# Two of sixteen row gathers per step split in two by the expert's number

## The reference

```python
q = (x @ w_query).reshape(B, T, H, 2, 128)                 # H = 8 heads
s1 = einsum('bthd,nd->bthn', q[..., 0, :], sub_keys_1)     # 128 keys each
s2 = einsum('bthd,nd->bthn', q[..., 1, :], sub_keys_2)
v1, i1 = top_k(s1, 16); v2, i2 = top_k(s2, 16)
cand_s = v1[..., :, None] + v2[..., None, :]
cand_e = i1[..., :, None] * 128 + i2[..., None, :]
top_s, top_pos = top_k(cand_s, 16)
experts = take_along_axis(cand_e, top_pos)                 # 16 of 16384
g = softmax(top_s)
u = expert_down[e]
hdn = gelu(einsum('chkd,cd->chk', u, x))
y = einsum('chk,chkd->cd', g * hdn, expert_up[e])
```

## Time and profile before

| | |
|---|---|
| Median of 3 runs | 864.57 us (864.12 to 865.37) |
| Span of the profiled execution, the time that the sums are made against | 862.9 us |
| PE busy | 755.6 us (88%) |
| DVE busy | 564.1 us (65%) |
| ACT busy | 180.2 us (21%) |
| POOL busy | 575.1 us (67%) |
| Moved by DMA | 308.39 MB, of it 268.47 MB by GpSimd's gathers |

### The profile page before, as it was taken

One profiled execution on the slowest core, in us unless ns is written; L12 is line 12 of the kernel. 1 busy time (PEld: TensorE's weight loads), 2 busy tenths in 40 slices (PEclk: granted clock), 3 DMA queues, 4 the chain that ended last, 5 costly groups with the idle time before them and its releaser, 6 DMA issues.

```text
span 862.9 us, 9305 instructions
## 1 busy us (share of the span) xinstructions
PE 755.6 (88%) x2473; PEld 390.9 (45%) x2473; DVE 564.1 (65%) x1503; ACT 180.2 (21%) x563; POOL 575.1 (67%) x716
## 2 busy tenths in 40 slices
PE   9999999999999879788888888888879797777786
PEld 6988668556554424244333434343434242222232
DVE  3565686239999667676767676666676666765445
ACT  2134455211212021122202030202020202112021
POOL 6886451017767777777777777777777777777770
PEclk9999999999999999999999999999999999999999
DMA  8948450659999999999999999999999999999997
GB/s 304 232 133 243 156 236 5 242 243 363 409 380 410 409 409 409 410 409 410 409 409 410 410 410 409 410 409 409 410 410 410 409 410 409 410 410 410 409 409 292
DMA packets 99487, 308.39 MB, mean 357 GB/s; under 512 B 18504, under 2 KB 23424, under 8 KB 99456
## 3 DMA queue, kind: packets, MB, share of 16 engines
q0 software_dynamic: 73728, 268.47, 78.3%
q1 hardware_dynamic: 24656, 39.39, 13.8%
q10 hardware_dynamic: 1072, 0.16, 0.1%
HBM read 306.41 MB, written 1.05 MB: 356 GB/s over the span
## 4 chain that ended last, share of the span: by engine, by line
PE 27%; DMA 27%; POOL 24%; issue 12%; DVE 8%; ACT 1%; DVEq 0%; ACTq 0%
PE bank L1530 24%; POOL region_w L647 18%; DMA region_w<-in_expert_up,chosen 14%; DMA region_w<-in_expert_down,chosen 11%; POOL gates L647 3%; DMA pool_bd<-in_expert_down,chosen 2%; PE xn_ps L1530 2%; PE bank L1533 2%; DVE region_w L1392 1%; POOL dn_spare L647 1%; POOL pool_bd L647 1%; DMA dn_spare<-in_expert_down,chosen 1%; DVE gates L1392 1%; DVE pool_bd L1392 1%; DVE region_q L1166 0%
## 5 line engine op out<-in xcount | busy, mean ns | idle before, releaser
L1530 PE MATMUL bank<-region_w,pool_bd 128*128 128x512 f32 (+2 forms) x1006 | 473.1, 598 | 96.6 <-DMA region_w<-in_expert_up,chosen 89.2
L1530 PEld LDWEIGHTS bank<-region_w,pool_bd 128*128 128x128 f32 x1006 | 174.4, 189 | 366.4 <-issue 294.5
L647 POOL DMA_INDIRECT region_w<-in_expert_up,chosen x250 | 234.8, 939 | 82.7 <-issue 61.4
L1392 DVE CUSTOM_DVE_ANT_0 region_w<-xn_ps,region_w 128x1024 f32<-128x1024 f32 x128 | 156.6, 1224 | 101.4 <-DMA region_w<-in_expert_down,chosen 101.0
L647 POOL DMA_INDIRECT region_w<-in_expert_down,chosen x128 | 120.6, 943 | 40.8 <-issue 32.9
L1392 DVE CUSTOM_DVE_ANT_0 gates<-xn_ps,gates 128x1024 f32<-128x1024 f32 x64 | 78.1, 1223 | 36.7 <-DMA gates<-in_expert_down,chosen 33.1
L908 ACT ACTIVATE pool_bd<-ident,pool_bd 128x128 f32<-128x128 f32 x251 | 78.4, 389 | 77.2 <-PE bank L1530 53.8
L647 POOL DMA_INDIRECT gates<-in_expert_down,chosen x64 | 60.4, 943 | 23.4 <-issue 16.5
L711 ACT ACTIVATE pool_bd<-bank 128x256 f32<-128x256 f32 (+3 forms) x49 | 19.0, 389 | 265.5 <-PE bank L1530 241.3
L1530 PE MATMUL bank<-region_q,oT 128*128 (+1 forms) x240 | 54.3, 379 | 0.0
L1392 DVE CUSTOM_DVE_ANT_0 dn_spare<-xn_ps,dn_spare 128x1024 f32<-128x1024 f32 x32 | 39.2, 1224 | 18.8 <-DMA dn_spare<-in_expert_down,chosen 18.6
(11 more groups left out here) (289 smaller groups left out, 786.8 us busy)
## 6 DMA issues: line engine op xcount, KB each, us to landing
region_q<-in_w_in SPq DMA_DIRECT2D x4, 2048.0 KB, 8.4
region_q<-in_w_query SPq DMA_DIRECT2D x1, 6144.0 KB, 23.9
region_w<-in_expert_up,chosen POOLq DMA_INDIRECT x250, 13.9
region_w<-in_w_out SPq DMA_DIRECT2D x1, 3072.0 KB, 20.9
x_sb<-in_x SPq DMA_DIRECT2D x4, 512.0 KB, 4.0
region_q<-in_w_in SPq DMA_DIRECT2D x2, 1024.0 KB, 11.4
region_q<-in_w_in SPq DMA_DIRECT2D x16, 128.0 KB, 3.0
region_w<-in_wb_nsa SPq DMA_DIRECT2D x2, 1024.0 KB, 16.6
```

The lines of the kernel that those rows point to most:

```text
L647: pool.indirect_dma_start(out=row, out_offset=None, in_=table, in_offset=bass.IndirectOffsetOnAxis(ap=of_slot(chosen, s, k), axis=0)).then ...
L1392: dve.tensor_tensor_reduce(out=row, in0=xn_ps[:, :], in1=row, scale=1.0, scalar=0.0, op0=ALU.mult, op1=ALU.add, accum_out=hdn[:, k:k + 1]) ...
L1530: return pe.matmul(out_, lhsT, rhs, start=start, stop=stop)
```

## The change

The down rows of ranks 7 and 15 (the last place of the ring, `APART`) are fetched in steps 0 to 14 by two gathers instead of one. Both go to the same buffer and count on the same semaphore. The first uses the old list of numbers with the bound 12287: rows of experts up to there are fetched, the others are left out. The second uses a list of its own, `chosen_high`, in which each number under 12288 has 65536 added, and the bound 16383: it fetches just the rows that the first left out. It is issued six downs later (`BEHIND`), after GpSimd has waited for the first one's landing. The dot waits for both. VectorE makes the second list by three small operations for each of the two ranks. In step 15 (`LAST`) all gathers are single as before. The semaphore counts of that place are changed to fit.

```diff
+APART = RING - 1
+BEHIND = 6
+LOW_KEYS = 96
+LOW_ROWS = LOW_KEYS * NK
+BEYOND = 65536.0
...
+        chosen_high = sb("chosen_high", STEPS * 2, U32)
+        high_f = sb("high_f", 4)
...
+        def high_of(s, k):
+
+            return chosen_high[:, bass.ds(s * 2 + k // RING, 1)]
...
-            return (dn_in if low else up_in)[slot], 16 * count
+            return (dn_in if low else up_in)[slot], 16 * (count + (2 * LAST if low and slot == APART else 0))
...
+            def part(index, bound):
+                pool.indirect_dma_start(
+                    out=ring_dn[APART], out_offset=None, in_=a["expert_down"],
+                    in_offset=bass.IndirectOffsetOnAxis(ap=index, axis=0),
+                    bounds_check=bound, oob_is_err=False).then_inc(dn_in[APART], 16)
...
                 if n >= RING:
                     pool.wait_ge(dn_used, n - RING + 1)
-                gather(ring_dn[k % RING], dn_in[k % RING], a["expert_down"], k, s)
+                if k % RING != APART or s == LAST:
+                    gather(ring_dn[k % RING], dn_in[k % RING], a["expert_down"], k, s)
+                else:
+                    part(of_slot(chosen, s, k), LOW_ROWS - 1)
+                first = n - BEHIND
+                if 0 <= first < LAST * SLOTS and first % RING == APART:
+                    pool.wait_ge(dn_in[APART], 32 * (first // RING) + 16)
+                    part(high_of(first // SLOTS, first % SLOTS), NK * NK - 1)
...
+            def high(p, k):
+
+                own.mark(dve.tensor_scalar(out=high_f[:, 0:1], in0=r12[:, 0, k:k + 1], scalar1=float(LOW_KEYS), scalar2=BEYOND,
+                                           op0=ALU.is_lt, op1=ALU.mult))
+                own.mark(dve.scalar_tensor_tensor(out=high_f[:, 1:2], in0=r12[:, 0, k:k + 1], scalar=float(NK), in1=r12[:, 1, k:k + 1],
+                                                  op0=ALU.mult, op1=ALU.add))
+                own.wait()
+                link(dve.tensor_tensor(out=high_of(p, k), in0=high_f[:, 0:1], in1=high_f[:, 1:2], op=ALU.add))
...
                 own.wait()
+                high(p, ranks.stop - 1)
...
+                for k in (RING - 1, SLOTS - 1):
+                    high(p, k)
                 dve.scalar_tensor_tensor(out=of_step(chosen, p), in0=r12[:, 0, :], scalar=float(NK), in1=r12[:, 1, :],
                                          op0=ALU.mult, op1=ALU.add).then_inc(chosen_ready, 1)
...
-            OWN_TURN = 27
+            OWN_TURN = 33
...
-                dve.wait_ge(dn_in[k % RING], (2 * s + k // RING + 1) * 16)
+                turn_ = 2 * s + k // RING + 1
+                if k % RING == APART:
+                    turn_ = turn_ + 2 * LAST if s is LAST else turn_ * 2
+                dve.wait_ge(dn_in[k % RING], turn_ * 16)
```

## The result

The changed kernel takes 994.44 us, median of three runs (993.35 to 994.61), where the kernel before takes 864.57: a ratio of 1.1495 [1.1475, 1.1516], slower by 130 us. The direction was as predicted and the mechanism too, but the size was not: 919 us were predicted and 948 was the upper end. The profiled execution has a span of 992.6 us.

The account below looks back on a forecast made before the run. Before, turns were DMA-bound at 410 GB/s; now the chain binds. d39 at 285.3 + 26 x 22.04 = 858.3, plus 46.9 to the last issue; end 54.4 later, span 917.3, so 919 us; range 886 to 948.

Parts of the forecast that it names:

- The chain: Across GpSimd, DMA and VectorE: first part, 12 gathers, second part, its landing, dot, next first part, with no slack.
- The first turns: Before the steady turns: late dots bring d39 (down gather 39, counted from d0) to about 285 us, where it was 268.35.
- The turn: One round of eight gather pairs: 16.16 + 4.1 + 1.34 + 0.44 = 22.04 us, where it was 20.5.
- L: Second part's time from issue to landing: 4.4 less 0.5 plus 0.2, 4.1 us; bounds 3.1 and 5.6.
- gathers ahead of it still being served, plus 0.2: In the second part's landing time: earlier gathers still on the DMA engines add 0.2 us.
- About 0.1 to start it and let GpSimd go.: Around the late row's dot on VectorE: starting it and releasing GpSimd adds about 0.1 us to its 1.23.
- 13 x 1.243: GpSimd's issues from first to second part: 13 gathers at 1.243 us each, 16.16 us a turn.
- the 0.87 behind slot 15: After a step's last dot, VectorE's other work makes GpSimd lose 0.87 us every second turn, 0.44 on average.
- The DMA engines carry the same bytes.: For the 30 extra gathers: splitting a gather in two adds no bytes for the DMA engines.
- dearer parts: Rival, chance 0.14: skipped rows cost about like real ones, each part 0.3 to 0.6 us dearer; 937 to 955 us.
- is not held: The up gather needing the slot TensorE frees late comes 13.7 us behind the next first part; no wait, costed at nothing.
- The backlog: DMA queue behind GpSimd's issues: it can't build now; last landing lag 5.6 us instead of 16.3, paying back 10.7.

Follow-up runs that it names:

- 7, 6 and 5 pairs: The changed kernel with the second part issued 7, 6 (no edit) or 5 pairs of gathers behind the first: 1068.76, 991.52 and 917.91 us.
- 3 pairs: The changed kernel with the second part issued 3 pairs of gathers behind the first instead of 6: 895.89 us, 1.036 of the kernel before.

## Why the prediction was wrong

The prediction's span was 917.3 us and the trace has 992.6, 75.3 more. By its own steps:

- **The chain.** Right, and shown by the slope with 7, 6 and 5 pairs and by the waits that move with it.
- **The first turns.** d39 was predicted at 285.3. GpSimd's timeline has the first parts of d7, d15, d39 and d239 at

```profile
200.89 1.00 POOL L663 DMA_INDIRECT region_w<-in_expert_down,chosen  x1 [0.30 <-issue]
...
219.76 1.00 POOL L663 DMA_INDIRECT region_w<-in_expert_down,chosen  x1 [3.60 <-DVE pool_bd L1431]
...
291.13 1.00 POOL L663 DMA_INDIRECT region_w<-in_expert_down,chosen  x1 [2.63 <-DVE pool_bd L1431]
...
907.97 1.00 POOL L663 DMA_INDIRECT region_w<-in_expert_down,chosen  x1 [2.88 <-DVE pool_bd L1431]
```

d15 is where it was said to be (219.7), d39 5.8 us later. The second parts of the two turns between went out at 260.28 and 283.77, where 258.7 and 279.5 were predicted.
- **The turn**, 22.04 predicted, (907.97 - 291.13) / 25 = 24.67 measured. This is the step that failed: 2.63 x 26 = 68.4 us. With the 5.8 it makes 74.2 of the 75.3. As means of the 25 turns, the timelines have 16.92 us from first to second part (16.16 + 0.44 predicted), 5.63 to the dot (4.1), 1.23 for the dot, and 0.90 to the next first part (0.11): 0.3 + 1.5 + 0.8 us. The mechanism was right, and two terms of the sum, *L* and the restart, were too small.
  - *L*, "a whole gather with idle DMA engines ... less 0.5 ... plus 0.2 = 4.1". It is 5.3 to 5.8 over the stages, median 5.6, the bound that I had kept for the far end: +1.5. Of its terms, "gathers ahead of it still being served, plus 0.2" looks like the wrong one. The row of 4.7 us had nothing ahead of it, but the second part is issued behind a train of gathers at 1.24 us each, and such gathers take 6 us to land even where no backlog grows (6.1 with 3 pairs). "Less 0.5" for the fewer rows was too small, if anything (0.8 to 0.9). Taken from a row in the train, it would have been 6.1 - 0.9 = 5.2.
  - *"About 0.1 to start it and let GpSimd go."* The dot ends at 515.46 and the first part starts at 516.26, 0.80 us later, and 414.03 to 414.83 and 439.11 to 439.91 at two others: +0.7. Once, up to 366.40, it was 3.20 us, and no run shows why. No row of before showed a long wait of GpSimd for a dot, and I took the price from none. It is not the bounded form: with one late plain gather a down gather starts 0.79 us behind its dot (its end at 528.93, the gather at 529.72), though an up gather there starts 0.27 behind (526.39 to 526.66). What makes the difference stays open.
  - *13 x 1.243*: a part is 1.00 us and not 0.94, so +0.06, and most turns have 16.25 and 16.95 in alternation. That looks like 16.16 with the 0.87 behind slot 15, but the agreement is in part luck. The rows of that step give 0.83, and in the turn shown GpSimd waits only 0.07 and 0.21 us beyond the usual 0.30 behind slot 15. The other 0.43 is the up gather at 503.47, which took 1.37 us and not 0.94; such a gather stands in nearly every second turn, and its cause is open.
  - The remaining 0.3 is mostly in single turns: a wait of 3.9 us for TensorE ahead of 460.02, waits of 1.8 and 1.9 ahead of 607.64 and 803.60, and GpSimd's own small operations ahead of 433.09.
- **"The DMA engines carry the same bytes."** Right for what they move (308.42 MB), though 15.73 MB more are read. It cost nothing here. The rival *dearer parts* came nearest with its sum (937 to 955 us), still 39 us short, and its mechanism is refuted: 30 whole parts in place of plain gathers cost 0.8 us, and left-out rows give 7.2 back.
- **TensorE "is not held".** Nearly: its waits cost GpSimd 15.3 us in 38 places, against 18.1 in 47, with a longest of 3.9.
- **The backlog** did not build (landings of 6.2 us, median, of the up rows), as said.
- **The Trainium skill's fit** (DMA: Bandwidth & Descriptors, Anatomy of one DMA) for a DMA from GpSimd is 2.0 us, setup and completion included, plus the bytes over 436 GB/s. These gathers take longer. For the whole gather on idle DMA engines the fit gives an estimate of 3.2 us and the trace has 4.7; for the first part issued at 516.26, some 96 rows, an estimate of 2.9 and the trace has 3.9; for the second part of 508.89, some 32 rows behind a train of gathers, an estimate of 2.3 and the trace has 5.3. With 2.3 for *L* the sum would have been further off than with 4.1.

## What to carry to other kernels

Before a fetch is moved later, close the loop: if its consumer frees the slot that the issuing engine waits for, then issue, landing, use and restart are one chain, and every one of them is paid in full in every turn. Take the landing time from a transfer in the same traffic as the moved one, not from the first transfer of a run, and the restart after a long wait from such a wait. And ask what a dry queue loses: before, a backlog hid landings of 18 us, and one wait of about 3 us per turn destroyed it.

## What the runs showed that I had not expected

- **A gather's left-out rows count as read, but are not carried.** 15.73 MB more in the read counter of the changed kernel; where a quarter of single gathers was left out, 4.17 MB less moved and 7.2 us faster; 9 ns of a DMA engine for a packet of 4 bytes against 162 for a row.
- **The transfers came back slowly after a gap.** Windows of the changed kernel over one turn (after the six figures of the engines: PEclk, DMA share, GB/s):

```profile
504.00:508.00 4.00, 4.00 (x11) 1.83 (x10) 1.86 (x4) 0.00 (x0) 3.08 (x4) 1.00 1.03 412
...
517.00:518.00 1.00, 1.00 (x4) 0.30 (x2) 1.00 (x3) 0.00 (x0) 0.70 (x2) 1.00 0.25 74
518.00:520.00 2.00, 2.00 (x5) 0.68 (x4) 1.97 (x5) 0.00 (x0) 1.44 (x2) 1.00 0.76 207
520.00:524.00 4.00, 1.31 (x3) 0.63 (x3) 3.93 (x15) 0.00 (x0) 3.03 (x4) 0.89 0.83 281
524.00:528.00 4.00, 3.75 (x7) 1.14 (x6) 3.73 (x11) 0.00 (x0) 3.08 (x4) 0.69 0.93 347
528.00:532.00 4.00, 2.86 (x10) 1.17 (x9) 0.86 (x3) 0.00 (x0) 3.09 (x4) 1.00 1.03 420
```

They run dry at 517 us and are at the full rate again only in the window from 528, although GpSimd issues without a wait from 516.26 on. At a share of 0.83 and 0.93 the engines are counted busy at 281 and 347 GB/s, where a share of 1.03 goes with 412. This leaves a small queue ahead of the second part and may be why landing is 5.6 us and not 5.2, as with 3 pairs; it was not isolated.
- **TensorE's granted clock fell after its waits.** It is 0.79 in the window from 314 to 355 us, in which TensorE is busy 29 of 41 us, and 1.00 there before with 34.6: part of the time at 1.2 and not 2.4 GHz. In the windows above it is 1.00 up to 520; TensorE then waits 2.69 us for rows, up to 522.79, and the next two windows have 0.89 and 0.69. What that costs was not measured. GpSimd, whose queue the chain runs through, waited 15.3 us for TensorE in all, and TensorE itself 113.2 us in 14 waits for the diagonals.
